# mLSTM sample outputs: one accumulation in 64 columns of the PE array, or two in its two 64-column halves

## The reference

```
# per head, for each sample sequence s with its own carried state C_s (256 x 256) and n_s (256)
sc  = (q_s k_s^T) * dw
num = sc v_s + w_prev * (q_s C_s)
den = sum(sc) + w_prev * (q_s . n_s)
h   = num / max(|den|, exp(-m))
C_s' = dec * C_s + (k_s * wk)^T v_s
```

## Time and profile before

| | |
|---|---|
| median of 3 runs | 2403.24 us (2398.9 to 2405.14) |
| profiled execution | 2400.85 us, span 2399.1 us |
| PE busy | 1850.0 us (77%) |
| DVE busy | 1526.0 us (64%) |
| ACT busy | 999.5 us (42%) |
| `mlstm` | about 453 to 627 us of the span |
| line 1480 (state products of the sample queries) | x128, 29.8 us busy, 391 ns each |
| line 1302 (new sample states) | x64, 27.6 us busy, 481 ns each |

### The profile page before, as it was taken

One profiled execution on the slowest core, in us unless ns is written; L12 is line 12 of the kernel. 1 busy time (PEld: TensorE's weight loads), 2 busy tenths in 40 slices (PEclk: granted clock), 3 DMA queues, 4 the chain that ended last, 5 costly groups with the idle time before them and its releaser, 6 DMA issues.

```text
span 2399.1 us, 29635 instructions
## 1 busy us (share of the span) xinstructions
PE 1850.0 (77%) x10264; PEld 1027.7 (43%) x10264; DVE 1526.0 (64%) x3503; ACT 999.5 (42%) x2544; POOL 670.1 (28%) x608
## 2 busy tenths in 40 slices
PE   7988799898698688888888887776666666666666
PEld 5765786566596445555544343332111111111110
DVE  3137453387555687777778776677666676666754
ACT  3231223121244455566544654445443444344443
POOL 0023000000000243433433344344434343444442
PEclk9989899899799899999998988888766676677766
DMA  4230522222653699999999999999999999999996
GB/s 161 79 114 9 178 70 71 73 76 100 214 175 111 252 414 415 415 414 415 414 407 415 416 399 419 418 419 416 420 421 420 416 414 420 420 420 418 416 416 272
DMA packets 168059, 741.01 MB, mean 309 GB/s; under 512 B 15985, under 2 KB 46773, under 8 KB 94056
## 3 DMA queue, kind: packets, MB, share of 16 engines
q0 software_dynamic: 82944, 604.02, 60.9%
q1 hardware_dynamic: 84968, 135.14, 16.7%
HBM read 719.55 MB, written 16.66 MB: 307 GB/s over the span
## 4 chain that ended last, share of the span: by engine, by line
DMA 38%; PE 15%; ACT 7%; DVE 5%; issue 2%; POOL 0%; ACTq 0%; POOLq 0%; DVEq 0%
DMA lower<-in_experts,upper 36%; PE bank L2338 8%; PE bank L1869 6%; DVE lower L2186 3%; DMA upper<-in_experts,upper 1%; ACT upper L2261 1%; ACT upper L2257 1%; ACT L2254 1%; PE bank L1866 1%; ACT upper L2254 1%; ACT L2240 1%; ACT upper_w_split L1663 0%; DVE upper_w_split L1748 0%; DVE lower L2201 0%; DVE upper L2186 0%
## 5 line engine op out<-in xcount | busy, mean ns | idle before, releaser
L2338 PE MATMUL bank<-lower,upper 64*64 64x512 f32 x4016 | 713.1, 796 | 346.6 <-ACT upper L2261 345.0
L2186 DVE SCALAR_TENSOR_TENSOR lower<-lower 128x1024 f32<-128x1024 f32 x502 | 614.4, 1224 | 331.4 <-DMA lower<-in_experts,upper 330.2
L2114 POOL DMA_INDIRECT lower<-in_experts,upper x502 | 549.1, 1094 | 784.1 <-PE bank L2338 758.4
L2338 PEld LDWEIGHTS bank<-lower,upper 64*64 64x64 f32 x4016 | 128.9, 159 | 813.8 <-ACT upper L2261 773.1
L1869 PEld LDWEIGHTS bank<-upper_x_split,upper_w_split 128*128 128x128 f32 x2688 | 390.1, 201 | 192.0 <-issue 110.7
L1869 PE MATMUL bank<-upper_x_split,upper_w_split 128*128 128x320 f32 (+1 forms) x2688 | 432.8, 316 | 50.3 <-DVE upper_w_split L1748 39.2
L2254 ACT ACTIVATE upper<-upper 128x1 f32<-128x1 f32 x576 | 115.6, 201 | 612.1 <-DVE lower L2186 521.1
L2114 POOL DMA_INDIRECT upper<-in_experts,upper x74 | 84.2, 1137 | 743.7 <-DVE upper L2168 595.6
L269 PE MATMUL bank<-upper_w_split,upper_x_split 128*128 128x512 f32 (+1 forms) x912 | 216.5, 399 | 11.2 <-DVE upper_w_split L251 11.0
L2261 ACT ACTIVATE upper<-lower,upper 128x64 f32<-128x64 f32 x576 | 200.4, 348 | 19.1
L269 PEld LDWEIGHTS bank<-upper_w_split,upper_x_split 128*128 128x128 f32 (+1 forms) x912 | 167.4, 185 | 59.3 <-DVE upper_w_split L251 13.7
(11 more groups left out here) (260 smaller groups left out, 1851.2 us busy)
## 6 DMA issues: line engine op xcount, KB each, us to landing
upper<-in_w_in SPq DMA_DIRECT2D x40, 512.0 KB, 3.6
lower<-in_w_pq SPq DMA_DIRECT2D x64, 256.0 KB, 7.6
lower<-in_w_in SPq DMA_DIRECT2D x64, 256.0 KB, 7.9
lower<-in_w_in SPq DMA_DIRECT2D x24, 512.0 KB, 3.7
upper<-in_state_C SPq DMA_DIRECT2D x8, 1024.0 KB, 7.6
out_C_s<-upper SPq DMA_DIRECT2D x16, 512.0 KB, 4.0
lower<-in_experts,upper POOLq DMA_INDIRECT x502, 15.6
lower<-in_x_prompt SPq DMA_DIRECT2D x8, 512.0 KB, 7.8
```

The costliest lines, as they stand in the source:

```text
L2114: pool.indirect_dma_start(ring[place(n)], None, I["experts"], bass.IndirectOffsetOnAxis(numbers[:, g, k:k + 1], 0)).then_inc(arrived[place ...
L2186: dve.scalar_tensor_tensor(out=u, in0=u, scalar=1.0, in1=xn2[:, tile_of(g), :], op0=ALU.mult, op1=ALU.mult, accum_out=dots[:, g % 2, k:k + ...
L2338: ins = pe.matmul(sums_of(c)[i][j * QUAD:(j + 1) * QUAD, :], diag[half, n % NDIAG, :], ring[place(n)][half, D + j * GRP:D + (j + 1) * GRP] ...
```

## The change

The 16 state matmuls are parted by the parity of s. Those of even s go on into partitions 0 to 63 of bank 0, as all did; those of odd s are accumulated in partitions 64 to 127 of the same bank, which are computed by the other 64 columns of the array. The two kinds alternate in the order on PE. After ACT has copied the even sum, a new DVE operation adds the odd sum to it. It stands at the head of `sample_state(h)` for heads 0 to 2, and before `divide(NCH)` for head 3.

```diff
-    sample_y = bank[0][0:NS, P:P + NE]
+    sample_y = [bank[0][half * NS:(half + 1) * NS, P:P + NE] for half in range(2)]
...
-                act.activation(yb_s[0:NS, h], sample_y, ACT.Copy).then_inc(S["ys_copied"], 1)
+                act.activation(yb_s[0:NS, h], sample_y[0], ACT.Copy).then_inc(S["ys_copied"], 1)
...
+            def add_odd(h):
+
+                dve.wait_ge(S["ys_copied"], h + 1)
+                chain.then(dve.tensor_tensor(yb_s[0:NS, h], yb_s[0:NS, h], sample_y[1], ALU.add))
+
             def sample_state(h):
 
                 dve.wait_ge(S["y_s"], h + 1)
+                if h < H - 1:
+                    add_odd(h)
...
             weighed_scores(NCH - 1)
+            add_odd(H - 1)
             divide(NCH)
...
-                pe.matmul(sample_y, prob_s[0:NS, h], v[0:NS, NCH, h, :], start=True, stop=False)
-                for s in range(NB):
+                pe.matmul(sample_y[0], prob_s[0:NS, h], v[0:NS, NCH, h, :], start=True, stop=False)
+                for pair in range(NB // 2):
                     for e in range(2):
-                        ins = pe.matmul(sample_y, qz[:, e, s], Cs[:, h % 2, s, e], start=False, stop=s == NB - 1 and e == 1)
+                        for half in range(2):
+                            s = 2 * pair + half
+                            ins = pe.matmul(sample_y[half], qz[:, e, s], Cs[:, h % 2, s, e], start=half == 1 and pair + e == 0,
+                                            stop=s + 2 >= NB and e == 1)
                 ins.then_inc(S["y_s"], 1)
```

## The result

The changed kernel takes 2391.98 us (median of 6 runs, 2390.2 to 2394.53); the kernel before, beside it on the same chip, 2400.43 us (6 runs). The ratio is 0.9964, 95% interval 0.9953 to 0.9975: 8.5 us less. The forecast was 2394.2, 9.0 us less than 2403.24, the median of three runs that it started from. In shares that is 0.36% less measured and 0.37% forecast.

A forecast was written before the change was run, and what follows sets the result against it. The prediction took the sample output on PE to bound the `mlstm` block. A saving of 10.8 us less 1.8 us for the additions gave -9.0 us, from 2403.24 to 2394.2 us, range 2389.5 to 2401.0.

The forecast's parts named there:

- What bounds the block: In `mlstm`, the sample output on PE is on the path in all four heads; what the block loses moves all behind.
- Part 1, the halves overlap: In each head's state matmuls on PE, two 64-column halves run side by side: 3.55 us for 7.10.
- estimate by the Trainium skill: State matmuls take 4.5 us instead of 3.55 per head; same sum as the partial-overlap rival, -7.5 us, chance 0.12.
- Part 2, what the saving is worth: Of 3.55 us saved per head on PE, 1.9, 3.3, 3.3 and 2.3 arrive in heads 0 to 3: 10.8 us.
- line 1416 also needs `diag_a`: Behind the sample output in heads 0 to 2, PE waits for line 1186, leaving savings of 1.9, 3.3 and 3.3 us.
- In head 3, which has no line 1424, the forecast: Before `divide(NCH)`, DVE loses its whole idle time of 2.30 us and no more, and pays 0.45 for the addition.
- Head 0's saving was given back: Rival: inside `mlstm` PE meets one or two more half-clock stretches, 1.7 us each; sum -3 to -6 us; chance 0.15.
- Part 3, the additions: Four added DVE operations, one per head, cost 0.45 us each, all on the path: 1.8 us.
- With PE (line 1494) four banks ahead at most and waiting for DVE: In heads 0 to 2 DVE runs back to back around the addition, so its 0.45 us is not hidden.

The follow-up runs named there:

- e4: The change with the eight matmuls of the even sequences first, then the eight of the odd, not alternating: 2398.79 us, ratio 0.9987 to the kernel before.
- e5: The change with line 1293 (DVE making kz) moved behind `running_max` of the next chunk, head 3's behind `divide(NCH)`: 2393.05 us, ratio 0.9957 to the kernel before.
- e9: The change with two halves in heads 1 and 2 only, heads 0 and 3 in one accumulation without addition: 2396.82 us, ratio 0.9989 to the kernel before.
- e10: The change plus four idle-work matmuls on PE behind head 0's state matmuls, filling its wait: 2392.05 us, ratio 0.9966 to the kernel before.
- e2: The change with 15 of each head's 16 state matmuls in the first half, the last in the second, additions kept: 2400.05 us, ratio 0.9993 to before.
- e3: The change without the four DVE additions, leaving out the odd sequences' state part: 2392.78 us, ratio 0.996 to the kernel before.
- e7: The kernel before with alternating 32-column stationary operands, each sequence's rows in its own part, no additions: 2393.05 us, ratio 0.9957 to the kernel before.
- e8: The kernel before with 32-column parts without additions and line 1293 moved behind `running_max`: 2392.57 us, ratio 0.996 to the kernel before.
- e6: The kernel before, in one accumulation, with only line 1293 moved behind `running_max`: 2404.41 us, ratio 1.0008 to the kernel before.
- e1: The changed kernel run once more, unaltered: 2393.05 us, ratio 0.9968 to the kernel before.
- e11: e10 plus five more idle-work matmuls on PE behind `spread_m` of each chunk: 2397.34 us, ratio 0.9987 to the kernel before.

## Why the prediction was right

**What bounds the block: right.** The sample output stood on the path in heads 1, 2 and 3, and in head 0 too as far as line 1199. The forecast left out DVE's second wait of heads 1 and 2 (3.15 us for ACT's copies), which does no harm, since it hangs on line 1424 as well. The shift passed on to the end whole: -8.98 in the block, 9.6 in the span.

**Part 1, the halves overlap: right,** 3.69 us for 7.17, as line 2308 said, and 15.7 us busy in all four heads where some 15 were forecast. The forecast's estimate by the Trainium skill (TensorE: Matmul & The Clock Gate, Part 3) was 4.5; this trace does not bear it out. e4 adds a condition that the forecast did not state: only because the halves alternate in the program.

**Part 2, what the saving is worth: 10.8 us forecast, 8.7 seen** (1.14, 2.64, 2.64 and, in head 3, 2.26 with the addition's 0.45 put back). The step that failed is "line 1416 also needs `diag_a`" (1424 in the kernel after). It also waits for `probs`, line 1260, which is 0.6 us later, a wait in `spread_a` of the code that was read over. With it goes 0.7 us in each of heads 0 to 2, 2.1 in all. Line 1199's three waits are 1.38, 1.28 and 1.28 us, 3.9 in all, where 1.9 was forecast. e5 bears it out: there line 1260 comes sooner, and line 1424 follows at once in head 0; and where the clock stayed full, in head 2, the path is shorter by 2.19. In head 3, which has no line 1424, the forecast was exact: 1.81 net against 1.85.

**Head 0's saving was given back,** which the forecast had as a rival and placed elsewhere. PE's new wait of 2.2 us was followed by a half-clock stretch over the outputs of chunk 0. It took the 1.14 us and 0.1 more. Shown by e9 (no halves in head 0, no stretch, same time from there on) and e10 (wait filled, no stretch, 1.35 us sooner). Why the clock fell after the wait stays open.

**Part 3, the additions: mis-sized,** nothing in head 0 and 0.05 to 0.07 us each in heads 1 and 2 instead of 0.45, since PE's products pace the updates behind them (e2, e3, e7). "With PE (line 1494) four banks ahead at most and waiting for DVE" was the wrong reading: DVE waited for PE in pieces so small that the list by line gives only 0.6 us for all 64 updates. Only head 3's is paid in full (0.46 here, 0.48 between e5 and e8): 0.6 us in all instead of 1.8.

**What made the sum come out.** In heads 1 and 2 the stretch from line 1199 to line 1224 was 0.85 us shorter each, for which the forecast has no term. The kernel before has half-clock stretches there, on `turn_k` and `spread_m`; the kernel after has full clock there, and so have e2, e4 and e6 behind heads 1 and 2, of which e6 has no second half at all. Line 1224 behind head 1, before and after, and the clock after:

```profile
543.62 0.16 DVE L1224 TENSOR_TENSOR upper<-upper,bank 128x4 f32<-128x4 f32 x1 [1.46 <-PE bank L1452]
...
540.52 0.16 DVE L1224 TENSOR_TENSOR upper<-upper,bank 128x4 f32<-128x4 f32 x1 [0.56 <-PE bank L1460]
```
```profile
538.50:542.00 3.50, 2.83 (x15) 1.73 (x14) 2.90 (x10) 0.21 (x1) 0.00 (x0) 1.00 0.94 320
```

So it doesn't come of the second half; it is how the stretches fell in the one profile of the kernel before, and whether they fall so in its other executions isn't known. The terms: heads +0.13, -2.64, -2.64, -1.81; clock twice -0.85; a last 0.3 in the turns. The time itself, -8.5 and -8.2 in two comparisons, says that the net is near the forecast's -9.0. That it came out so near is in part luck: two errors, 2.1 (line 1260) and 1.2 (additions), pull opposite ways, and so do two effects of the clock that the sum has no term for, 1.3 lost behind head 0 and 1.7 gained on `turn_k` and `spread_m`.

## What to carry to other kernels

Narrow stationary operands that follow each other on the same columns can be laid side by side, if their order alternates; a second sum to be added is not always needed: e7 lays the rows out so that it has none. Before counting a saving whole, read every wait of the next instruction on that engine and not only the one that the profile shows now, since the profile shows the last alone. And an engine that finishes early waits, and on PE that wait can be followed by a slower clock. Moving other work out of the way (e5, e8) moved the wait, and the slow clock with it. Around head 2, what bounds the changed kernel is DVE's own work ahead of line 1260, line 1293 with it, and no longer the sample output (e5, 2.19 us).

## What the runs showed of the hardware

Parts of 64 and of 32 columns run in pairs at the price of one record, 3.69 and 3.68 us for 32 records of 257 columns. PE starts records of one part beside earlier ones of the other out of the program's order, but not far: in e4 four pairs overlapped where eight matmuls (16 records) of each stood in a row.

A half-clock stretch on the path cost as much as the change's details are worth: 0.9 us at line 1224 (before), 1.35 behind head 0 (the change against e10), 1.67 on line 1551 (e5). Those behind head 0 followed a wait of 2.2 us, those on line 1551 one of 3.1, in every profile that has the wait. But not every such wait is followed by one: in e5 PE waits 2.68 us ahead of head 2's records, and these run at full clock (3.70 us). e3, e7 and e9 have one on head 3's records, the kernel after and e1 none; a filling that removed one in e10 moved one to a worse place in e11. None of the improvements of 1 to 3 us in the block (e5, e8, e10) could be told in the time.
